# Norms by row tile between the stages of a second transformer block, and one output tile between probabilities

## The reference

```python
h = _rms_norm(x, norm_mix_pre[i])
mixed = _attention_sublayer(...) if i % 2 == 0 else _deltanet_sublayer(...)
x = x + _rms_norm(mixed, norm_mix_post[i])
h = _rms_norm(x, norm_ffn_pre[i])
x = x + _rms_norm(_swiglu(h, ffn_w_gate_up[i], ffn_w_down[i]), norm_ffn_post[i])
```

## Time and profile before

| what | value |
|---|---|
| median of 3 runs | 2160.9 us (2159.92 to 2163.43) |
| the profiled execution's own time | 2167.4 us |
| its span | 2165.3 us |
| PE busy | 1905.4 us, 88% of the span |
| DVE busy | 592.1 us (27%) |
| ACT busy | 404.4 us (19%) |
| mean granted clock of PE | 0.95 of full speed |

### The profile page before, as it was taken

How to read it: one execution, slowest core, us unless ns; L and a number is a source line. 1 busy time by engine, 2 the same in 40 slices (tenths; PEclk the granted TensorE clock), 3 DMA queues, 4 the chain that set the end, 5 groups by cost and what they waited for, 6 DMA issues and landing times.

```text
span 2165.3 us, 24253 instructions
## 1 busy us (share of the span) xinstructions
PE 1905.4 (88%) x9681; PEld 1049.6 (48%) x9682; DVE 592.1 (27%) x1167; ACT 404.4 (19%) x584; POOL 61.4 (3%) x82
## 2 busy tenths in 40 slices
PE   6989997899998887889797779879999899979997
PEld 4744462233333222223232248538884577658863
DVE  4657242211222211221111122610000389520001
ACT  2230122121212221212222121210000235210000
POOL 2000010000000000000000010002001000000000
PEclk9999999999999998999998889989999999999999
DMA  9654758999999999999999990264440323064410
GB/s 315 221 181 174 260 200 351 427 429 383 417 428 428 427 428 428 427 419 390 428 428 427 428 389 19 83 247 112 147 148 16 127 78 127 33 249 155 150 65 20
DMA packets 106224, 574.45 MB, mean 265 GB/s; under 512 B 7271, under 2 KB 8803, under 8 KB 81552
## 3 DMA queue, kind: packets, MB, share of 16 engines
q1 hardware_dynamic: 102000, 563.46, 65.1%
q0 software_dynamic: 4160, 10.06, 1.7%
HBM read 572.42 MB, written 1.07 MB: 265 GB/s over the span
## 4 chain that ended last, share of the span: by engine, by line
PE 74%; DMA 13%; DVE 6%; ACT 4%; issue 2%; DVEq 0%; SPq 0%; ACTq 0%
PE ps L2004 14%; DMA ring<-in_w_up 12%; PE ps L1468 10%; PE ps L2015 7%; PE ps L1503 6%; PE ps L711 5%; PE ps L1482 4%; PE ps L1515 3%; PE ps L897 2%; PE ps L1492 2%; PE ps L719 2%; PE ps L2491 1%; PE ps L1022 1%; PE ps L1442 1%; PE ps L1093 1%
## 5 line engine op out<-in xcount | busy, mean ns | idle before, releaser
L2004 PE MATMUL ps<-arena,ring 128*128 128x256 f32 x1408 | 304.4, 379 | 1.8 <-issue 1.8
L2004 PEld LDWEIGHTS ps<-arena,ring 128*128 128x128 f32 x1408 | 267.4, 190 | 38.4 <-issue 2.1
L1503 PE MATMUL ps<-ring,arena 128*32 128x512 f32 x1216 | 162.0, 681 | 62.6 <-DMA ring<-in_w_up 62.4
L1468 PE MATMUL ps<-ring,arena 128*64 128x512 f32 x960 | 213.1, 595 | 0.0
L2015 PE MATMUL ps<-ring,arena 128*128 128x512 f32 x352 | 151.4, 592 | 0.0
L711 PE MATMUL ps<-arena,ring 128*128 128x256 f32 x608 | 132.8, 380 | 0.0
L1468 PEld LDWEIGHTS ps<-ring,arena 128*64 128x64 f32 x960 | 66.2, 137 | 134.2 <-issue 133.1
L711 PEld LDWEIGHTS ps<-arena,ring 128*128 128x128 f32 x608 | 115.0, 190 | 16.8 <-issue 1.5
L1503 PEld LDWEIGHTS ps<-ring,arena 128*32 128x32 f32 x1216 | 39.3, 123 | 171.9 <-issue 97.8
L1482 PE MATMUL ps<-ring,arena 128*64 128x512 f32 x480 | 106.3, 594 | 11.2 <-ACT arena L1431 11.2
L2015 PEld LDWEIGHTS ps<-ring,arena 128*128 128x128 f32 x352 | 66.9, 190 | 83.3 <-issue 83.2
(11 more groups left out here) (594 smaller groups left out, 2038.8 us busy)
## 6 DMA issues: line engine op xcount, KB each, us to landing
ring<-in_w_gate SPq DMA_DIRECT2D x64, 2048.0 KB, 18.8
ring<-in_w_up SPq DMA_DIRECT2D x64, 2048.0 KB, 22.2
ring<-in_w_down SPq DMA_DIRECT2D x64, 2048.0 KB, 19.1
ring<-in_ffn_w_gate_up SPq DMA_DIRECT2D x22, 2048.0 KB, 8.1
ring<-in_ada_w SPq DMA_DIRECT2D x12, 2048.0 KB, 11.7
ring<-in_ffn_w_down SPq DMA_DIRECT2D x10, 2048.0 KB, 7.9
ring<-in_w_in SPq DMA_DIRECT2D x8, 2048.0 KB, 21.3
ring<-in_dn_w_in SPq DMA_DIRECT2D x6, 2048.0 KB, 7.7
```

The lines of the kernel that those rows point to most:

```text
L1468: m = pe.matmul(bank(b)[c * CAP:(c + 1) * CAP, :], xT[:, j * P + h * CAP:j * P + (h + 1) * CAP], w[h][:, j, c * 512:(c + 1) * 512], start= ...
L1503: m = pe.matmul(bank(b)[(2 * i + c) * FEW:(2 * i + c + 1) * FEW, :], xT[:, j * P + h * CAP:j * P + h * CAP + FEW], w[h][:, j, c * 512:(c + ...
L2004: m = pe.matmul(bank(b0 + g)[:, c * SEQ:(c + 1) * SEQ], w[:, k, (2 * g + c) * P:(2 * g + c + 1) * P], hT2[:, k, :], start=(k == 0), stop=( ...
```

## The change

For q = 1 to 4 a seam is written row tile by row tile (`act_over_by_tile`, `dve_over_by_tile`). A new semaphore `first_ps` tells that tile 0's products are complete, and tile 0's norms start at it. To that end:

- in attention 2 the six sets of probabilities are no longer uniform: tile 1's three sets are transposed, then a part of tile 0's output product runs (8, 4 and 4 matmuls), then the set meets its values. The output product uses banks 0 to 3 in place of 4 to 7;
- the last two pieces of the down products run for all of tile 0 first, then for all of tile 1 (12 matmuls each), and need both pieces at the start;
- after the seam the first gate and up piece, and in the delta layer the gates and memory queries, are computed per row tile, so 128 moving columns at a time instead of 256: 64 matmuls in place of 32, and 32 in place of 16.

Tile 1's statistics now come from a square sum on ACT too, in place of DVE's `bn_stats`. On ACT, the copies of tile 0's turned bank stand behind tile 1's first root; on DVE, tile 0's other bank stands behind tile 1's scale and add.

```diff
+        def act_over_by_tile(act, o, q, b0, summed, written, junk, then):
+            for t in range(TT):
+                act.wait_ge(*(summed if t else (first_ps, q)))
+                o(act.activation(junk, bank(b0 + 2 * t, 2), ACT.Square, accum_out=ssq[:, t:t + 1]), sq_done)
+                act.wait_ge(ms_done, root_of(q, t))
+                o(act.activation(rms[:, t:t + 1], rms[:, t:t + 1], ACT.Sqrt), rt_done)
+                if q == 4:
+                    continue
+                if t:
+                    act_first_turned(act, o, q)
+                act.wait_ge(written[0], written[1] + t + 1)
+                o(act.activation(junk, x3[:, t, :], ACT.Square, accum_out=ssq2[:, t:t + 1]), sq_pre)
+                act.wait_ge(ms_pre, 2 * q + t + 1)
+                o(act.activation(rms2[:, t:t + 1], rms2[:, t:t + 1], ACT.Sqrt), rt_pre)
...
         def pe_ffn(pe, i):
-            pe_over(pe, 2 * i + 1)
-            pe_turned_on(pe, 2 * i + 1, 1)
+            pe_over(pe, q, (0,))
+            pe_turned_on(pe, q, 0)
+            first_gate_up(0, 0)
+            pe_over(pe, q, (1,))
+            first_gate_up(1, 0)
+            pe_turned_on(pe, q, 1)
+            first_gate_up(0, 1)
+            first_gate_up(1, 1).then_inc(gu_ps, 1)
...
+            for t in range(TT):
+                for n, w in last:
+                    for j in range(w.shape[1]):
+                        m = down(n, w, j, t)
+                    if t:
+                        m.then_inc(dn_ps, 1)
+                if t == 0:
+                    m.then_inc(first_ps, 1)
...
+            for g, part in enumerate(((0, 0, KD), (1, 0, KD // 2), (1, KD // 2, KD))):
+                pe_probs_turned(pe, 9 + g)
+                if g == 0:
+                    ws = [arrived(pe, pc) for pc in pc_ao[0]]
+                    pe.wait_ge(pv_ev, 9)
+                    pe.wait_ge(sc_sub, 12)
+                m = out_of(0, *part)
+                if g == 2:
+                    m.then_inc(first_ps, 1)
+                pe_probs_values(pe, 9 + g, values_of(g))
             pe.wait_ge(pv_ev, 12)
-            pe_out(pe, 0)
+            out_of(1, 0, 0, KD).then_inc(out_ps, 1)
+            out_of(1, 1, 0, KD).then_inc(out_ps, 1)
...
+            pe_over(pe, 2, (0,))
+            pe_turned_on(pe, 2, 0)
+            gates(0)
+            memory_queries(0, 0)
+            pe_over(pe, 2, (1,))
+            memory_queries(1, 0)
+            pe_turned_on(pe, 2, 1)
+            gates(1)
+            memory_queries(0, 1)
+            memory_queries(1, 1).then_inc(proj_ps, 1)
```

More of the change, by code:

```diff
@@ L1817, in block_kernel, with root_of, act_first_turned @@
         diag = [ar(6144 + P * t, P) for t in range(TT)]
+        first_ps = sem("first_ps")
+        def root_of(q, t):
+            return FIRST_ROOTS + 2 * q + t
+        def act_first_turned(act, o, q):
+            act.wait_ge(turn_ps, turn_base(PRE[q]) + 1)
+            for k in range(4):
+                o(act.activation(hT2[:, k, 0:P], bank(0)[:, k * P:(k + 1) * P], ACT.Copy, scale=pre_g[:, q, k:k + 1]),
+                  turned if k == 3 else None)
+        def act_over_by_tile(act, o, q, b0, summed, written, junk, then):
[12 more added lines that the diff above has]
+                o(act.activation(rms2[:, t:t + 1], rms2[:, t:t + 1], ACT.Sqrt), rt_pre)
+            if q < 4:
+                o(act.activation(dummy, con("ones")[:, 0:1], then))
@@ L2006, in pe_ffn, with down @@
                 m.then_inc(gu_ps, 1)
[L2007 removed]
+            def down(n, w, j, t):
+                f = 4 * n + j
+                for d in range(2):
+                    m = pe.matmul(bank(2 * t + d), actF[:, f, t * P:(t + 1) * P], w[:, j, d * 512:(d + 1) * 512],
+                                  start=(f == 0), stop=(f == FC2 - 1))
+                return m
+            for n, pc in enumerate(pc_dn[i][:4]):
                 w = arrived(pe, pc)
[L2009 to L2012, removed]
+                if n == 0:
+                    pe.wait_ge(gu_done, 11 * i + 10)
+                for j in range(4):
                     for t in range(TT):
[L2014 to L2016 removed]
+                        m = down(n, w, j, t)
                 m.then_inc(dn_ps, 1)
+            last = [(n, arrived(pe, pc_dn[i][n])) for n in (4, 5)]
+            pe.wait_ge(gu_done, 11 * i + 11)
+            for t in range(TT):
+                for n, w in last:
+                    for j in range(w.shape[1]):
+                        m = down(n, w, j, t)
+                    if t:
+                        m.then_inc(dn_ps, 1)
+                if t == 0:
+                    m.then_inc(first_ps, 1)
         def act_ffn(act, o, i):
@@ L2533, in pe_chunks @@
             within(1, 6)
-            out_of(0, 1, ws[1])
+            out_of(0, 1, ws[1]).then_inc(first_ps, 1)
             pe.wait_ge(on_ready, 2)
```

88 lines of the change are left out of this document (61 added, 27 removed).

## The result

| | before | after |
|---|---|---|
| median, same chip | 2160.41 us (4 runs) | 2142.05 us (4 runs, 2137.23 to 2146.27) |
| ratio, 95% interval | | 0.9916 [0.9893, 0.9939] |
| profiled execution, its span | 2167.4, 2165.3 us | 2137.2, 2135.1 us |
| mean granted clock of that execution | 0.950 | 0.956 |

Predicted were 2132.7 us and 2125 to 2139. The time lies 3 us outside: faster, as forecast, but by 18.4 us where 28.2 were expected; the interval of the ratio allows 13.2 to 23.1 us.

The account below looks back on a forecast made before the run. PE was taken to bound the kernel, with breaks at the seams. Gains of 9.2 + 8.1 + 7.5 + 3.5 + 5.3 = 33.6 us, less 5.4 for the clock, gave 28.2 and 2132.7 us, range 2125 to 2139.

Parts of the forecast that it names:

- Step 1: Seam: PE's first gate product starts 5.47 us after the last product, waiting for tile 0's turned bank, not a diagonal.
- Step 2: Seams: tile 0's 7.06 us chain is hidden beside tile 1's products; PE idles 3.7 us in place of 8.9.
- Step 4: Attention 2: ACT's copies run beside output products, from the transposes of set 9 to the last product; gain 5.3 us.
- Rival C: Attention 2: output weights come late, eating all of step 4's gain; time 2138.0 us, chance 0.03.
- Rival D: Seams: tile 0's chain is not done when tile 1's products end; no change, 2160.9 us; chance 0.02.
- Step 3: The four seams at full clock: gains of 9.2, 8.1, 7.5 and 3.5 us, with narrow products at 0.109 us each.
- Rival E: Narrow products paced by weight loads: slower, 2165.7 us at 0.212 us each, deciding from 0.197 on; chance 0.02.
- Step 5: Clock falls at each of three seams, 3.6 us of work at half speed: 1.8 us lost each, 5.4 in all.
- rival B: Half clock lasts as long as in the old first seam: 9.3 us lost in all, time 2136.6 us; chance 0.09.
- What else moves: Weight pieces, bn_stats leaving DVE and DVE's copies of values around the seams: all costed at nothing.
- The step from the profile to the median: Whole kernel: the profiled execution lies 6.5 us above the median of 2160.9; the same 28.2 us gain was taken from the median.

Follow-up runs that it names:

- before_2: The kernel before, unedited, profiled a second time: that profile took 2169.96 us, where 11 executions on its chip had a median of 2159.83 us.
- Warm: Changed kernel plus four unread 512-column products filling PE's idle time at each of three seams: 2137.45 us, ratio 0.9888 to the kernel before.
- attn: The kernel before with only attention 2's new order, old seams kept: 2157.46 us, ratio 0.9979 to the kernel before.
- quiet: Changed kernel with two transfers (output weights, gain) issued only after the delta layer's 144 small products: 2139.20 us, ratio 0.9903 to the kernel before.
- swap: Changed kernel with DVE copying tile 0's turned bank before tile 1's scale and add: 2134.61 us, ratio 0.9882 to the kernel before.
- seams: Changed kernel with attention 2's old order, so only the seams by row tile: 2148.29 us, ratio 0.9946 to the kernel before.

## Why the prediction was right in direction and wrong in size

**Steps 1, 2 and 4 held.** The first gate product at T + 5.46 (5.47 forecast), PE idle for 3.7 us, three times, and for the turned bank; no wait for a diagonal of tile 1; the last add's end at T + 4.6 (4.65 forecast). Tile 0's diagonal was there 8.4 us before T in the first seam, in the timeline after:

```profile
1429.31 0.29 DVE L1866 TENSOR_SCALAR arena<-constants,smalls 128x128 f32<-128x128 f32 x1
```

Attention 2 gained 5.2 us of 5.3 forecast; against before_2 it is 6.5, so that the two agree to 0.1 is luck. Rivals C and D fell with these rows: the output product started directly behind the transposes, and tile 0's chain was hidden.

**Step 3's pitch was nearly right.** Narrow products at full clock take 10.72 / 96 = 0.1117 us, 0.0027 more than I took. Over the 400 narrow and turning instructions of three seams that is 1.1 us. Rival E needed 0.197 and fell. The Trainium skill ("TensorE: Matmul & The Clock Gate", section "The mechanism") says that a weight load overlaps a running matmul only where their row groups differ. This trace does not agree at this width either: 0.112 us per instruction, with a load of 0.19 us by its own row.

**Step 5 was the term mis-sized.** The clock did fall at all three seams, though at the third only when PE was back. I took the shortest low stretches of before, 3.6 us of work or 1.8 us lost per seam. By the first 32 products of each seam against 32 x 0.1117 = 3.57 us it cost 6.42 - 3.57 = 2.8, 3.58 + 3.25 - 3.57 = 3.3 and 5.44 - 3.57 = 1.9 us: 8.0 in all, where the sum has 5.4. That is between my term and rival B's 9.3. Warm shows that it is the clock: with PE kept busy it gave 7.2 us back at the three seams. I had rows of two seams and took the shortest stretches without a reason but nearness; two of three cases came nearer the longest. The second seam, which is not among the windows of the earlier trace rows, was the worst, and in before_2 its clock fell a second time behind the turning.

**"What else moves" failed for the delta layer.** I costed at nothing what lies between the seams. The stage behind seam q 2 became 2.9 us longer than in the first profile of before and 6.0 longer than in the second, by work at a low clock; why the clock is lower there stays open. The new stall of 2.7 us, which shrinks or goes when the list or the transfers are shifted, is replaced by other waits when it goes, and is not shown to be the cause. That the stall would come could not be read from the trace of before, where the row of this kind is 0.3 us; that a stage can vary by this much could, had I looked at more than one profile: the same stage, from the second T on, took 215.4 us in one profile of before, 216.5 in the other and 211.4 in attn, where only a few semaphore waits in it differ.

With these, 28.2 - 2.6 (clock) - 1.1 (narrow products) - 2.9 (delta layer) - 0.1 (attention 2) + 0.4 (the FFNs) = 21.9 us, against 22.1 measured.

**The step from the profile to the median failed too.** I wrote that nothing of these stages was tied to the 6.5 us by which the profiled execution lay above the median, and took the whole difference from the median. Both profiles of before lie at the slow end of their kernel: 2167 and 2170 us at a clock of 0.950, each above every run beside it. Among the 17 runs of one chip, those under 2160 us have clocks of 0.952 to 0.957 and those over 2164 us 0.947 to 0.950. The low stretches at the seams, which the change shortens, enter that clock, but no profile shows whether they are shorter in a median execution. After's profile is, at 2137.23, its kernel's fastest run. Of the 30.2 us between the two profiled executions, 6.8 lie ahead of attention 2, where nothing was changed, and 23.4 in the own stages; the medians differ by 18.4, and 23 is the edge of the interval. The last 4 to 5 us are therefore put down to which two executions were compared; that is argued. It could be before's own stages, which may be shorter in a median execution: attn's profile, its kernel's fastest run, has the stages it shares with before 4 us shorter. The changed kernel's own stages were 853.8 and 854.5 us in executions 8.3 us apart. No profile fell on a median execution of before, so it stays open.

## What to carry to other kernels

When a seam's long wait is taken away, look in the order of each queue for what the freed engine will stand for next: here 3.7 us three times for one copy queued behind another tile's adds. Moving that copy was worth some 8 us, and turning the first tile inside the second one's products 13, about as much as the seams' part of the change. Work behind a gap of 4 us can run at half pace, so a gap is priced by its length and by the pace of the products behind it, taken from several gaps and not from the mildest. And a sum made from one profile is compared with that profile's place in the spread of its kernel before it is taken from a median.

## What was not expected of the hardware

- The clock fell in or just behind idle gaps of 3.7 us (4.1, 5.0 and 5.7 us after the last wide product), and the work behind ran at half pace for 3.7 to 6.5 us (twice what was lost; granted clock 0.67, 0.54 and 0.69 in the windows above), the same in two executions. In kernel quiet the third gap, of the same length, had no low clock behind it, and in swap one of 1.6 us was followed by a low clock over 8.9 us of work. Moving 16 small products back moved the low stretch and kept it.
- PE stood for 2.7 us amid 32x32 products with no engine to wait for, in the same place in two executions and in seams, 0.3 to 1.2 us in four other kernels with small edits elsewhere, and not at all in quiet, where 2.5 MB of transfers started later. Two kernels without the change, before_2 and attn, have no such stop either.
- The same 5934 PE instructions ahead of attention 2 took 1281.3 to 1291.4 us in different executions, with PE busy from 1086.5 to 1100.9 us.
